# Layer 0: two units of products run one after the other, or interleaved by contraction tile

## The chip, the cores and the metric

One Trainium2 chip, one core of it. The metric is the device time of one execution of the whole program in microseconds (us), the median of several runs. Engines are named as the profile names them: PE is TensorE (PEld its weight loads), ACT is ScalarE, DVE is VectorE, POOL is GpSimd, SP is SyncE, which here issues nearly all DMAs.

## What is computed

A two-layer decoder trunk on 256 tokens of width 1024, in float32. Only the start of layer 0 matters here:

```python
xn = rms_norm(h, norm_mix_g[layer])
proj = xn @ ab_w_in[j]          # (256 x 1024) @ (1024 x 2560)
u_pool = proj[..., :256]
q, k   = the next 2 x 768 columns
v      = the last 768 columns
```

Then come pooling, six heads of differential attention, an output projection and a dense SwiGLU block; layer 1 has the same shape. All weights are read once from device memory, about 104 MB in all, so weights stream in during the whole program.

## The kernel before

**Slabs.** The host packs the weights into slabs of 128 partitions x 2048 floats (1 MB). A slab passes three places. SP loads it into one of `RAW_SLOTS = 3` raw buffers, taken in turn, so slab n can only be issued once slab n-3 has left its buffer (`sp.wait_ge(lo_ready, n-2)` in `load`). ACT rounds it to the matmul format, `w_hi` (`split_hi`, L574; parts of a slab in `part_his`, L587). DVE makes the remainder `w_lo = raw - w_hi` (`split_lo`, L1046; `part_los`, L1061) and counts `lo_ready`, which frees the raw buffer. A product takes three matmuls: hi x hi, lo x hi, hi x lo. ACT, DVE and SP each run their instructions strictly in program order; semaphore waits stand in front of the instructions that need them.

**The first two units.** `first_unit(0, 4)` makes the first 512 columns of v from slabs 0 and 1 (contraction tiles k = 0 to 3 in slab 0, 4 to 7 in slab 1) into PSUM banks 4 and 5, one per half of the tokens. `first_unit(2, 6)` makes the pool columns and the last 256 columns of v from slabs 2 and 3 into banks 6 and 7. Each step (one unit, one k) is six matmuls of 512 columns: two with `w_hi` (L1791), two with the token remainder (L1795), two with `w_lo` (L1798).

**Small pieces at the start.** Slabs 0 and 1 are loaded as three pieces of 512 columns and two of 256 (`load_first`); slabs 2 and 3 as two halves of 1024. The token columns for k = 1 to 7 come in between on the same queue (x columns: k = 1, k = 2 and 3, k = 4 to 7), and ACT (`cols_his`, L594) and DVE (`cols_los`, L1078) split them too.

**What follows.** On SP: slabs 2 to 5, the two halves of the input `h` (L499), `params`, slabs 6 to 9. On PE after the two units: `first_qk_chunk` with slabs 4 and 5, in it `rstd_rows` and `pool_transposes` (L2005), which waits for ACT to have copied the four banks 4 to 7 out (`nat_copied`, the last copy is L696). On ACT the order is slabs 4 and 5, four squares of `h` (L611), slab 6, and then those copies (L691 to L696).

Of the kernel before, what the change touches and what calls it, by code (L numbers as in the profile page):

```python
# [42 lines left out]
HALVES = 2  # L43
# [115 lines left out]
def trunk(nc, x, x_cols, norm_mix_g, norm_ffn_g, norm_final_g, params_in, slabs, out):  # L159
# [45 lines left out]
    with ctx:  # L205
# [237 lines left out]

        def part_no(s, p=0):

            return FIRST_PARTS * s + p + 1 if s < FIRST_SLABS else FIRST_SLABS * (FIRST_PARTS - 1) + s + 1

        block = ctx.enter_context(nc.Block())

# [1 line left out]
        @block.sync  # L451
        def _(sp):
            def load(n):

                key, r, free = loads[n]
                for what, count in free or ():
                    sp.wait_ge({"lo": lo_ready, "forms": forms_ready, "sum": block_sum}[what], count)
                for b in range(2):
                    c = slice(b * SLAB // 2, (b + 1) * SLAB // 2)
                    own = n < PARTED and b == 0  # L460
                    sp.dma_start(raw_of(r, c), slabs[n, :, c])\
                        .then_inc(half_loaded[n - FIRST_SLABS] if own else raw_loaded[r], 16)

            def load_first(s):

                for p in range(FIRST_PARTS):
                    c = slice(p * 512, (p + 1) * 512)
                    sp.dma_start(raw[:, s, c], slabs[s, :, c]).then_inc(first_loaded[FIRST_PARTS * s + p], 16)
                    if s == 0 and p == 0:
                        sp.dma_start(x_rest[:, 1, :], cols_of[:, 1, :]).then_inc(cols_loaded[1], 16)  # L470
                    if s == 0 and p == 1:
                        sp.dma_start(x_rest[:, 2:4, :], cols_of[:, 2:4, :]).then_inc(cols_loaded[2], 16)
                for c0 in range(FIRST_PARTS * 512, SLAB, 256):
                    sp.dma_start(raw[:, s, c0:c0 + 256], slabs[s, :, c0:c0 + 256]).then_inc(raw_loaded[s], 16)
                if s == 0:
                    sp.dma_start(x_rest[:, 4:KC, :], cols_of[:, 4:KC, :]).then_inc(cols_loaded[3], 16)

            def load_gain(st):
                g = [norm_ffn_g[0:1, :], norm_mix_g[1:2, :], norm_ffn_g[1:2, :], norm_final_g][st - 1]
                if st > 1:  # L480
                    sp.wait_ge(normed, norm_no(st))
                sp.dma_start(gain[:, :], g.broadcast_to([P, D])).then_inc(gain_loaded, 16)

            def load_all(l, part):
                for n, (key, r, free) in enumerate(loads):
                    if key[1] == l and (key[0] if key[0] in ("mix", "out") else "ffn") == part:
                        if n < FIRST_SLABS:
                            load_first(n)
                        else:
                            load(n)  # L490
                        if n == NAT[0] + 1:
                            load_x()
                            sp.dma_start(params[:, :], params_in).then_inc(params_loaded, 16)

            def load_x():

                sp.wait_ge(cols_lo, KC)
                for half in range(HALVES):
                    sp.dma_start(h[:, half, :], x[half * P:(half + 1) * P, :]).then_inc(x_loaded[half], 16)  # L499

            for l in range(2):
                load_all(l, "mix")
                load_gain(2 * l + 1)
                load_all(l, "out")
                load_all(l, "ffn")
                load_gain(2 * l + 2)
            for b in range(2):
                c = slice(b * HALFD, (b + 1) * HALFD)
                sp.wait_ge((normed, last_scaled)[b], (norm_no(4) + 1, 1)[b])
                sp.dma_start(out[0:P, c], h[:, 0, c]).then_inc(out_stored, 16)  # L510
            sp.wait_ge(normed, norm_no(4) + 2)
            sp.dma_start(out[P:2 * P, 3 * D // 4:], h[:, 1, 3 * D // 4:]).then_inc(out_stored, 16)
            sp.wait_ge(normed, norm_no(4) + 3)
            sp.wait_ge(last_scaled, 2)
            sp.dma_start(out[P:2 * P, 0:3 * D // 4], h[:, 1, 0:3 * D // 4]).then_inc(out_stored, 16)
            sp.wait_ge(out_stored, 16 * 2 * HALVES)
# [45 lines left out]
        def _(act):  # L562
            A = nc.scalar.activation

            def split_hi(s):

                r, made = preps[s]
                if FIRST_SLABS <= s < PARTED:
                    part_his(s)
                act.wait_ge(raw_loaded[r], made)  # L570
                if s >= SLOTS:
                    act.wait_ge(slab_used, s - SLOTS + 1)
                c = slice((FIRST_PARTS * 512 if s < FIRST_SLABS else SLAB // 2) if s < PARTED else 0, SLAB)
                A(w_hi[:, s % SLOTS, c], raw_of(r, c), ACT.Copy).then_inc(hi_ready, 1)  # L574
# [108 lines left out]
            def mix0_act():  # L683
# [3 lines left out]
                split_his(6)  # L687
                for half in range(HALVES):
                    act.wait_ge(pow_done, pow_no("norm", 0, half))
                    act.wait_ge(slab_used, 2)  # L690
                    A(v[:, half, 0:512], bank[:, 4 + half, :], ACT.Copy, scale=rstd[:, half:half + 1])\  # L691
                        .then_inc(nat_copied, 1)
                for half in range(HALVES):
# [318 lines left out]
            act.dma_start(first_cols, x_cols[:, 0:KC + SEQ]).then_inc(cols_loaded[0], 16)  # L1012
            act.wait_ge(consts, 1)
            A(lam_t[:, 0:1], power[:, 0:1], ACT.Copy)
            for s in range(FIRST_SLABS):
                for p in range(FIRST_PARTS):
                    if s or p:
                        cols_his(4 * s + p)
                    part_his(s, p)
                cols_his(4 * s + FIRST_PARTS)  # L1020
                split_his(s)
            split_his(2, 3)
            mix0_act()
            ffn_act(0)
# [5 lines left out]
        def _(dve):  # L1030
# [8 lines left out]

            def split_lo(s):  # L1040

                if FIRST_SLABS <= s < PARTED:
                    part_los(s)
                dve.wait_ge(hi_ready, s + 1)
                c = slice((FIRST_PARTS * 512 if s < FIRST_SLABS else SLAB // 2) if s < PARTED else 0, SLAB)
                V.tensor_tensor(w_lo[:, s % SLOTS, c], raw_of(preps[s][0], c),  # L1046
                                w_hi[:, s % SLOTS, c].bitcast(F32), ALU.subtract).then_inc(lo_ready, 1)
# [671 lines left out]
                    last_columns()  # L1719

            V.memset(ones, 1.0).then_inc(ones_made, 1)
            for s in range(FIRST_SLABS):
                for p in range(FIRST_PARTS):
                    cols_los(4 * s + p)
                    part_los(s, p)
                cols_los(4 * s + FIRST_PARTS)
                split_los(s)
            split_los(2, 3)
            mix0_dve()
            ffn_dve(0)  # L1730
# [5 lines left out]
        def _(pe):  # L1736
# [13 lines left out]
            def w_part(s, c0, n):  # L1750
                return w_hi[:, slot(s), c0:c0 + n], w_lo[:, slot(s), c0:c0 + n]
# [18 lines left out]
                if not release:  # L1770
                    last.then_inc(done, 1)

            def first_unit(s, b0):

                def split_done(parted, done, t, k):

                    if t < FIRST_SLABS and k % 4 < FIRST_PARTS:
                        pe.wait_ge(parted, part_no(t, k % 4))
                    elif k % 4 == 0:
                        pe.wait_ge(parted, part_no(t))  # L1780
                    elif k % 4 == (FIRST_PARTS if t < FIRST_SLABS else 2):
                        pe.wait_ge(done, t + 1)

                for k in range(KC):
                    t = s + k // 4
                    w1, w2 = w_part(t, (k % 4) * 512, 512)
                    if s == 0:
                        pe.wait_ge(*((cols_hi, k) if k else (col0_hi, 1)))
                    split_done(part_hi, hi_ready, t, k)
                    for half in range(HALVES):  # L1790
                        T.matmul(bank[:, b0 + half, :], xT_hi[:, half, k, :], w1, start=k == 0, stop=False)  # L1791
                    if s == 0:
                        pe.wait_ge(cols_lo, k + 1)
                    for half in range(HALVES):
                        T.matmul(bank[:, b0 + half, :], xT_lo[:, half, k, :], w1, start=False, stop=False)  # L1795
                    split_done(part_lo, lo_ready, t, k)
                    for half in range(HALVES):
                        last = T.matmul(bank[:, b0 + half, :], xT_hi[:, half, k, :], w2, start=False, stop=k == KC - 1)  # L1798
                    if k % 4 == 3:
                        last.then_inc(slab_used, 1)  # L1800

            def rstd_rows():

# [243 lines left out]
            def mix(l):  # L2047
                st, m = 2 * l, mix0[l]
                if l == 0:
                    first_unit(0, 4)  # L2050
                    first_unit(2, 6)
                else:
                    unit(m, m, 0, 4, done=nat_done, st=st)
                    unit(m + 2, m + 2, 0, 5, done=nat_done, midway=lambda: norm_transposes(st, 1))
# [323 lines left out]
```

## Time and profile before

| | |
|---|---|
| median of 3 runs | 566.34 us (566.11 to 566.46) |
| the profiled execution | 566.4 us |
| its span in the trace | 564.1 us |
| PE busy | 556.9 us, 99% of the span |
| DVE, ACT, POOL busy | 461.9, 324.3, 15.5 us |

The 2.3 us between execution and span lie outside the program's instructions. A busy share is not a limit by itself; what ends a wait is. Times below are us from the start of the span.

### The profile page before, as it was taken

Reading aid. Unit: us, or ns where it says so; the run is one execution under the profiler, and the core shown is the slowest. Engines: PE = TensorE matmul, PEld = TensorE weight load, DVE = VectorE, ACT = ScalarE, POOL = GpSimd, SP = SyncE. Lnnn points to the kernel's source line nnn. Section 1 sums busy time; section 2 is a strip of 40 time slices with the busy share of each in tenths; the row PEclk is TensorE's granted clock in tenths of the full one; section 3 lists DMA queues with packets and bytes.
Section 4 is the critical chain, followed back from the end, with each engine's and each line's share of the span. In section 5 each row is a group of like instructions: output and inputs, shape, how many; then the busy total and the mean of one; then the engine's idle time right before and its main releaser. Section 6 shows DMA issues by size and latency. Waiting matters only on the chain.

```text
span 564.1 us, 7600 instructions
## 1 busy us (share of the span) xinstructions
PE 556.9 (99%) x2949; PEld 475.1 (84%) x2949; DVE 461.9 (82%) x571; ACT 324.3 (57%) x454; POOL 15.5 (3%) x55
## 2 busy tenths in 40 slices
PE   8999999999999999999999999999999999999995
PEld 7899978888888888888888888888888888888884
DVE  5679996776988789897797998977779887798875
ACT  6686864654564555556576356546475545555543
POOL 1200001000000000000000000000000000000000
PEclk9999999999999999999999999999999999999999
DMA  8975644455627394467479622445744464926431
GB/s 297 353 298 164 217 149 145 154 195 180 223 76 243 104 314 159 145 228 255 156 242 315 226 76 74 161 146 164 273 164 140 150 223 150 304 85 215 144 112 74
DMA packets 30419, 105.65 MB, mean 187 GB/s; under 512 B 3376, under 2 KB 4272, under 8 KB 30384
## 3 DMA queue, kind: packets, MB, share of 16 engines
q1 hardware_dynamic: 30240, 105.04, 54.3%
q8 instruction: 23, 0.38, 0.3%
q10 hardware_dynamic: 144, 0.14, 0.1%
q14 instruction: 12, 0.10, 0.0%
HBM read 104.11 MB, written 1.05 MB: 186 GB/s over the span
## 4 chain that ended last, share of the span: by engine, by line
PE 97%; DMA 1%; issue 1%; DVE 1%; SPq 0%; ACT 0%; POOLq 0%; POOL 0%; DVEq 0%
PE bank L1748 20%; PE bank L1746 20%; PE bank L1747 20%; PE bank L2179 13%; PE bank L2182 7%; PE bank L1844 4%; PE bank L1847 2%; PE bank L1791 1%; PE bank L1795 1%; PE bank L1798 1%; PE bank L1816 1%; DMA raw<-in_slabs 1%; PE bank L1936 1%; PE bank L2224 1%; PE bank L1962 0%
## 5 line engine op out<-in xcount | busy, mean ns | idle before, releaser
L1046 DVE TENSOR_TENSOR w_lo<-raw,w_hi 128x2048 fp32r<-128x2048 f32 (+2 forms) x92 | 204.8, 2228 | 35.7 <-ACT w_hi L574 35.7
L574 ACT ACTIVATE w_hi<-raw 128x2048 fp32r<-128x2048 f32 (+2 forms) x83 | 153.7, 1862 | 28.6 <-DMA raw<-in_slabs 26.4
L1746 PE MATMUL bank<-w_lo,yT_hi 128*128 128x512 f32 (+1 forms) x242 | 96.1, 397 | 0.0
L1748 PE MATMUL bank<-w_hi,yT_lo 128*128 128x512 f32 (+1 forms) x242 | 94.1, 389 | 0.0
L1747 PE MATMUL bank<-w_hi,yT_hi 128*128 128x512 f32 (+1 forms) x242 | 94.0, 388 | 0.0
L2179 PE MATMUL bank<-xT,w_hi 128*128 128x512 f32 x320 | 80.5, 393 | 0.0
L2179 PEld LDWEIGHTS bank<-xT,w_hi 128*128 128x128 f32 x320 | 57.8, 189 | 10.6
L1746 PE MATMUL bank<-w_lo,xT 128*128 128x512 f32 (+1 forms) x160 | 61.9, 387 | 0.0
L1748 PE MATMUL bank<-w_hi,xT 128*128 128x512 f32 (+1 forms) x160 | 60.8, 380 | 0.0
L1747 PE MATMUL bank<-w_hi,xT 128*128 128x512 f32 (+1 forms) x160 | 60.6, 379 | 0.0
L1748 PEld LDWEIGHTS bank<-w_hi,yT_lo 128*128 128x128 f32 x242 | 45.4, 188 | 9.6
L1746 PEld LDWEIGHTS bank<-w_lo,yT_hi 128*128 128x128 f32 x242 | 45.5, 188 | 8.5 <-DVE yT_lo L1262 0.2
L1747 PEld LDWEIGHTS bank<-w_hi,yT_hi 128*128 128x128 f32 x242 | 45.6, 188 | 8.3
L2182 PEld LDWEIGHTS bank<-xT,w_lo 128*128 128x128 f32 x320 | 43.6, 190 | 3.1
L2182 PE MATMUL bank<-xT,w_lo 128*128 128x256 f32 x320 | 44.6, 282 | 0.0
L581 ACT ACTIVATE w_hi<-raw 128x2048 fp32r<-128x2048 f32 x16 | 30.7, 1917 | 21.3 <-DVE raw L1577 21.3
L1577 DVE TENSOR_TENSOR raw<-raw 128x2048 f32<-128x2048 f32 x16 | 36.5, 2284 | 0.0
L1748 PEld LDWEIGHTS bank<-w_hi,xT 128*128 128x128 f32 x160 | 30.1, 188 | 5.8
L1747 PEld LDWEIGHTS bank<-w_hi,xT 128*128 128x128 f32 x160 | 30.1, 188 | 5.3
L1746 PEld LDWEIGHTS bank<-w_lo,xT 128*128 128x128 f32 x160 | 30.1, 188 | 5.2
L1746 PE MATMUL bank<-xT,w_hi 128*128 128x256 f32 x96 | 27.6, 287 | 0.0
L1748 PE MATMUL bank<-xT,w_lo 128*128 128x256 f32 x96 | 27.2, 283 | 0.0
(229 smaller groups left out, 840.8 us busy)
## 6 DMA issues: line engine op xcount, KB each, us to landing
raw<-in_slabs SPq DMA_DIRECT2D x170, 512.0 KB, 4.7
spare<-in_slabs SPq DMA_DIRECT2D x16, 512.0 KB, 5.3
raw<-in_slabs SPq DMA_DIRECT2D x6, 256.0 KB, 6.1
h<-in_x SPq DMA_DIRECT2D x2, 512.0 KB, 8.6
gain<-in_norm_ffn_g SPq DMA_DIRECT2D x2, 512.0 KB, 7.2
raw<-in_slabs SPq DMA_DIRECT2D x4, 128.0 KB, 5.5
h<-in_x_cols SPq DMA_DIRECT2D x1, 512.0 KB, 6.3
gain<-in_norm_mix_g SPq DMA_DIRECT2D x1, 512.0 KB, 5.7
```

What stands on the lines that cost most here:

```text
L574: A(w_hi[:, s % SLOTS, c], raw_of(r, c), ACT.Copy).then_inc(hi_ready, 1)
L581: A(w_hi[:, s % SLOTS, :], raw_of(preps[s][0]), ACT.Copy).then_inc(hi_ready, 1)
L1046: V.tensor_tensor(w_lo[:, s % SLOTS, c], raw_of(preps[s][0], c), w_hi[:, s % SLOTS, c].bitcast(F32), ALU.subtract).then_inc(lo_ready, 1)
L1577: V.tensor_tensor(o, p, q, ALU.subtract).then_inc(block_sum, 1)
L1746: T.matmul(o, st_hi, mv_lo, start=first, stop=False)
L1747: T.matmul(o, st_hi, mv_hi, start=False, stop=False)
L1748: return T.matmul(o, st_lo, mv_hi, start=False, stop=last)
L1791: T.matmul(bank[:, b0 + half, :], xT_hi[:, half, k, :], w1, start=k == 0, stop=False)
L1844: T.matmul(bank[:, b, :], hi, xT[:, k, :, :, :], start=k == 0, stop=False)
L1847: last = T.matmul(bank[:, b, 0:SEQ], lo, xT_hi[:, :, k, :], start=False, stop=k == KC - 1)
L2179: T.matmul(bank[:, b + m, :], hi, xT[:, k, :, :, :], start=k == 0, stop=False)
L2182: last = T.matmul(bank[:, b + m, 0:SEQ], lo, xT_hi[:, :, k, :], start=False, stop=k == KC - 1)
```

## The change

The two units run interleaved: for each k, first the step of the v unit, then the step of the other. So the slabs are packed in another order: slab 0 is v columns k = 0 to 3, slab 1 pool and second v columns k = 0 to 3, slab 2 v columns k = 4 to 7, slab 3 the others k = 4 to 7. The small pieces of slabs 0 and 1 are loaded in turn, and ACT and DVE prepare them in turn. In the second half, the first half of slab 3 is split ahead of the second half of slab 2.

```diff
-            def load_first(s):
+            def load_first():
                 for p in range(FIRST_PARTS):
                     c = slice(p * 512, (p + 1) * 512)
-                    sp.dma_start(raw[:, s, c], slabs[s, :, c]).then_inc(first_loaded[FIRST_PARTS * s + p], 16)
-                    if s == 0 and p == 0:
+                    for s in range(FIRST_SLABS):
+                        sp.dma_start(raw[:, s, c], slabs[s, :, c]).then_inc(first_loaded[FIRST_PARTS * s + p], 16)
+                    if p == 0:
                         sp.dma_start(x_rest[:, 1, :], cols_of[:, 1, :]).then_inc(cols_loaded[1], 16)
...
-            for s in range(FIRST_SLABS):          # DVE
-                for p in range(FIRST_PARTS):
-                    cols_los(4 * s + p)
-                    part_los(s, p)
-                cols_los(4 * s + FIRST_PARTS)
-                split_los(s)
+            for p in range(FIRST_PARTS):
+                cols_los(p)
+                part_los(0, p)
+                part_los(1, p)
+            cols_los(3)
+            split_los(0, 1)
+            cols_los(4)
+            part_los(2)
+            cols_los(5, 6, 7)
+            part_los(3)
             split_los(2, 3)
...
                 for k in range(KC):
+                    for u in range(2):
+                        t, b0 = u + 2 * (k // 4), 4 + 2 * u
...
                                         # mix0_act, before the copies of banks 4 and 5
-                    act.wait_ge(slab_used, 2)
+                    act.wait_ge(slab_used, 3)
...
-            slabs += v4 + [columns(k0, 4, (w_in, 0, 256), (w_in, c_v + 512, 256)) for k0 in (0, 4)]
+            for k0, t in zip((0, 4), v4):
+                slabs += [t, columns(k0, 4, (w_in, 0, 256), (w_in, c_v + 512, 256))]
```

ACT's sequence changes in the same way as DVE's (`part_his`, `cols_his`, `split_his`). The functions `split_hi` and `split_lo` no longer call `part_his` and `part_los` for slabs 2 and 3; these stand in the sequence itself.

The order of SP's first DMAs, before (raw pieces are slab pieces, h<-in_x_cols are token columns):

```order
L468 DMA raw<-in_slabs 128x512
L470 DMA h<-in_x_cols 128x256
L468 DMA raw<-in_slabs 128x512
L472 DMA h<-in_x_cols 128x512
L468 DMA raw<-in_slabs 128x512
L474 DMA raw<-in_slabs 128x256 x2
L476 DMA h<-in_x_cols 128x1024
L468 DMA raw<-in_slabs 128x512 x3
L474 DMA raw<-in_slabs 128x256 x2
L461 DMA raw<-in_slabs 128x1024 x8
```

And of the change:

```order
L469 DMA raw<-in_slabs 128x512 x2
L471 DMA h<-in_x_cols 128x256
L469 DMA raw<-in_slabs 128x512 x2
L473 DMA h<-in_x_cols 128x512
L469 DMA raw<-in_slabs 128x512 x2
L476 DMA raw<-in_slabs 128x256 x4
L477 DMA h<-in_x_cols 128x1024
L461 DMA raw<-in_slabs 128x1024 x8
```

The same thirteen DMAs go out ahead of slab 2, but the last pieces of slab 0 have moved behind three pieces of slab 1.

DVE from the last piece of slab 0 (the first L1046 row, which frees its raw buffer) to slab 3, before:

```order
L1046 TENSOR_TENSOR w_lo<-raw,w_hi 128x512 [waits hi_ready]
L1078 SCALAR_TENSOR_TENSOR xT<-h,rows,xT 128x256 [waits cols_hi]
L1061 TENSOR_TENSOR w_lo<-raw,w_hi 128x512 [waits part_hi]
...
L1046 TENSOR_TENSOR w_lo<-raw,w_hi 128x512 [waits hi_ready]
L1061 TENSOR_TENSOR w_lo<-raw,w_hi 128x1024 [waits part_hi]
L1046 TENSOR_TENSOR w_lo<-raw,w_hi 128x1024 [waits hi_ready]
L1061 TENSOR_TENSOR w_lo<-raw,w_hi 128x1024 [waits part_hi]
L1046 TENSOR_TENSOR w_lo<-raw,w_hi 128x1024 [waits hi_ready]
```

And of the change, from the same place:

```order
L1047 TENSOR_TENSOR w_lo<-raw,w_hi 128x512 [waits hi_ready] x2
L1079 SCALAR_TENSOR_TENSOR xT<-h,rows,xT 128x256 [waits cols_hi]
L1062 TENSOR_TENSOR w_lo<-raw,w_hi 128x1024 [waits part_hi]
L1079 SCALAR_TENSOR_TENSOR xT<-h,rows,xT 128x256 [waits cols_hi] x3
L1062 TENSOR_TENSOR w_lo<-raw,w_hi 128x1024 [waits part_hi]
L1047 TENSOR_TENSOR w_lo<-raw,w_hi 128x1024 [waits hi_ready] x2
L1047 TENSOR_TENSOR w_lo<-raw,w_hi 128x2048 [waits hi_ready] x2
```

The second half of slab 2 (before: the third row with L1046; in the change: the first of the two in the row L1047 128x1024 x2) now stands behind three token columns and the first half of slab 3.

## Rows read from the trace of the kernel before

**Rows 1.** The page: busy time, share and instructions of PE.

```profile
PE 556.9 (99%) x2949; PEld 475.1 (84%) x2949; DVE 461.9 (82%) x571; ACT 324.3 (57%) x454; POOL 15.5 (3%) x55
```

**Rows 2.** Waits of PE over the whole span: total us, times, longest.

```profile
PE bank L1742 <- DVE probT L1721: 1.0, 1, 1.0
PE bank L1791 <- ACT w_hi L587: 0.4, 1, 0.4
```

**Rows 3.** Timeline of PE, 5 to 29 us: start, duration, what.

```profile
5.23 0.86 PE L1791 MATMUL bank<-w_hi,xT 128*128 128x512 f32 x2
6.39 0.63 PE L1798 MATMUL bank<-w_lo,xT 128*128 128x512 f32 x2
...
7.46 0.70 PE L1791 MATMUL bank<-w_hi,xT 128*128 128x512 f32 x2 [0.44 <-ACT w_hi L587]
8.45 0.61 PE L1798 MATMUL bank<-w_lo,xT 128*128 128x512 f32 x2
9.14 0.70 PE L1791 MATMUL bank<-w_hi,xT 128*128 128x512 f32 x2
...
10.61 0.62 PE L1791 MATMUL bank<-w_hi,xT 128*128 128x512 f32 x2
...
28.31 0.28 PE L1746 MATMUL bank<-xT,w_hi 128*128 128x256 f32 x1
```

**Rows 4.** Timeline of ACT, 4 to 19 us, where it waits for DMAs.

```profile
6.68 0.63 ACT L587 ACTIVATE w_hi<-raw 128x512 fp32r<-128x512 f32 x1 [1.20 <-DMA raw<-in_slabs]
7.71 0.51 ACT L594 ACTIVATE xT<-h,rows 128x256 fp32r<-128x256 f32 x1 [0.40 <-DMA h<-in_x_cols]
8.37 0.63 ACT L587 ACTIVATE w_hi<-raw 128x512 fp32r<-128x512 f32 x1
...
11.01 0.63 ACT L587 ACTIVATE w_hi<-raw 128x512 fp32r<-128x512 f32 x1 [0.18 <-DMA raw<-in_slabs]
...
16.99 1.06 ACT L587 ACTIVATE w_hi<-raw 128x1024 fp32r<-128x1024 f32 x1 [0.21 <-DMA raw<-in_slabs]
```

**Rows 5.** Timeline of DVE, 10 to 21 us.

```profile
10.04 0.69 DVE L1046 TENSOR_TENSOR w_lo<-raw,w_hi 128x512 fp32r<-128x512 f32 x1
...
13.29 0.48 DVE L1078 SCALAR_TENSOR_TENSOR xT<-h,rows,xT 128x256 fp32r<-128x256 f32 x1
...
16.80 1.23 DVE L1046 TENSOR_TENSOR w_lo<-raw,w_hi 128x1024 fp32r<-128x1024 f32 x1
18.08 1.23 DVE L1061 TENSOR_TENSOR w_lo<-raw,w_hi 128x1024 fp32r<-128x1024 f32 x1
```

**Rows 6.** Timeline of SP: issues of slabs 3, 4, 5, input halves.

```profile
10.75 0.33 SPq L461 DMA_DIRECT2D raw<-in_slabs  x1
15.39 0.33 SPq L461 DMA_DIRECT2D raw<-in_slabs  x1
18.06 0.33 SPq L461 DMA_DIRECT2D raw<-in_slabs  x1
18.90 0.93 SPq L499 DMA_DIRECT2D h<-in_x  x2
```

**Rows 7.** DMA view at 15.3 to 15.6: issue to landing, first half of slab 4.

```profile
raw<-in_slabs SPq DMA_DIRECT2D x1, 512.0 KB, 4.1
```

**Rows 8.** Windows: busy us of each engine, granted clock, DMA share, GB/s.

```profile
9.00:16.00 7.00, 6.92 (x31) 5.71 (x31) 6.34 (x12) 6.18 (x13) 0.88 (x5) 1.00 1.05 405
20.00:24.00 4.00, 4.00 (x19) 3.30 (x18) 1.85 (x2) 1.92 (x1) 0.28 (x3) 1.00 0.95 299
24.00:30.00 6.00, 6.00 (x35) 5.26 (x34) 3.18 (x2) 3.98 (x8) 0.00 (x0) 1.00 1.02 388
```

**Rows 9.** Timeline, 20 to 38 us: slabs 4, 5, 6 on ACT and DVE, the copies, the transposes.

```profile
20.75 1.92 ACT L574 ACTIVATE w_hi<-raw 128x2048 fp32r<-128x2048 f32 x1 [1.46 <-DMA raw<-in_slabs]
25.86 1.92 ACT L574 ACTIVATE w_hi<-raw 128x2048 fp32r<-128x2048 f32 x1 [3.19 <-DMA raw<-in_slabs]
...
27.81 2.29 DVE L1046 TENSOR_TENSOR w_lo<-raw,w_hi 128x2048 fp32r<-128x2048 f32 x1 [2.82 <-ACT w_hi L574]
...
31.18 0.28 PE L1746 MATMUL bank<-xT,w_hi 128*128 128x256 f32 x1
...
32.26 1.92 ACT L574 ACTIVATE w_hi<-raw 128x2048 fp32r<-128x2048 f32 x1 [1.54 <-DMA raw<-in_slabs]
...
36.29 0.50 ACT L696 ACTIVATE v<-bank,rstd 128x256 f32<-128x256 f32 x1
...
37.15 0.60 PE L2005 MATMUL bank<-ident,u_sb 128*128 128x128 f32 x4
```

More of the change, by code:

```diff
@@ L444, in part_no @@
         def part_no(s, p=0):
-            return FIRST_PARTS * s + p + 1 if s < FIRST_SLABS else FIRST_SLABS * (FIRST_PARTS - 1) + s + 1
+            return FIRST_SLABS * p + s + 1 if s < FIRST_SLABS else FIRST_SLABS * (FIRST_PARTS - 1) + s + 1
         block = ctx.enter_context(nc.Block())
@@ L462, in load @@
                         .then_inc(half_loaded[n - FIRST_SLABS] if own else raw_loaded[r], 16)
-            def load_first(s):
+            def load_first():
                 for p in range(FIRST_PARTS):
                     c = slice(p * 512, (p + 1) * 512)
-                    sp.dma_start(raw[:, s, c], slabs[s, :, c]).then_inc(first_loaded[FIRST_PARTS * s + p], 16)
-                    if s == 0 and p == 0:
+                    for s in range(FIRST_SLABS):
+                        sp.dma_start(raw[:, s, c], slabs[s, :, c]).then_inc(first_loaded[FIRST_PARTS * s + p], 16)
+                    if p == 0:
                         sp.dma_start(x_rest[:, 1, :], cols_of[:, 1, :]).then_inc(cols_loaded[1], 16)
-                    if s == 0 and p == 1:
+                    if p == 1:
                         sp.dma_start(x_rest[:, 2:4, :], cols_of[:, 2:4, :]).then_inc(cols_loaded[2], 16)
[L473 to L476, printed above, removed]
+                for s in range(FIRST_SLABS):
+                    for c0 in range(FIRST_PARTS * 512, SLAB, 256):
+                        sp.dma_start(raw[:, s, c0:c0 + 256], slabs[s, :, c0:c0 + 256]).then_inc(raw_loaded[s], 16)
+                sp.dma_start(x_rest[:, 4:KC, :], cols_of[:, 4:KC, :]).then_inc(cols_loaded[3], 16)
             def load_gain(st):
@@ L486, in load_all @@
                     if key[1] == l and (key[0] if key[0] in ("mix", "out") else "ffn") == part:
-                        if n < FIRST_SLABS:
-                            load_first(n)
-                        else:
+                        if n == 0:
+                            load_first()
+                        elif n >= FIRST_SLABS:
                             load(n)
@@ L567, in split_hi @@
                 r, made = preps[s]
-                if FIRST_SLABS <= s < PARTED:
-                    part_his(s)
                 act.wait_ge(raw_loaded[r], made)
@@ L1014, in _ @@
             A(lam_t[:, 0:1], power[:, 0:1], ACT.Copy)
-            for s in range(FIRST_SLABS):
-                for p in range(FIRST_PARTS):
[L1017 to L1021, printed above, removed]
+            for p in range(FIRST_PARTS):
+                if p:
+                    cols_his(p)
+                part_his(0, p)
+                part_his(1, p)
+            cols_his(3)
+            split_his(0, 1)
+            cols_his(4)
+            part_his(2)
+            cols_his(5, 6, 7)
+            part_his(3)
             split_his(2, 3)
@@ L1040, in split_lo @@
             def split_lo(s):
-                if FIRST_SLABS <= s < PARTED:
-                    part_los(s)
                 dve.wait_ge(hi_ready, s + 1)
@@ L1721, in _ @@
             V.memset(ones, 1.0).then_inc(ones_made, 1)
-            for s in range(FIRST_SLABS):
-                for p in range(FIRST_PARTS):
-                    cols_los(4 * s + p)
-                    part_los(s, p)
-                cols_los(4 * s + FIRST_PARTS)
-                split_los(s)
+            for p in range(FIRST_PARTS):
+                cols_los(p)
[7 more added lines that the diff above has]
+            part_los(3)
             split_los(2, 3)
@@ L1771, in unit, with first_units @@
                     last.then_inc(done, 1)
-            def first_unit(s, b0):
+            def first_units():
                 def split_done(parted, done, t, k):
@@ L1784, in first_unit @@
                 for k in range(KC):
[L1785 to L1800, printed above, removed]
+                    for u in range(2):
+                        t, b0 = u + 2 * (k // 4), 4 + 2 * u
+                        w1, w2 = w_part(t, (k % 4) * 512, 512)
+                        if u == 0:
+                            pe.wait_ge(*((cols_hi, k) if k else (col0_hi, 1)))
+                        split_done(part_hi, hi_ready, t, k)
+                        for half in range(HALVES):
+                            T.matmul(bank[:, b0 + half, :], xT_hi[:, half, k, :], w1, start=k == 0, stop=False)
+                        if u == 0:
+                            pe.wait_ge(cols_lo, k + 1)
+                        for half in range(HALVES):
+                            T.matmul(bank[:, b0 + half, :], xT_lo[:, half, k, :], w1, start=False, stop=False)
+                        split_done(part_lo, lo_ready, t, k)
+                        for half in range(HALVES):
+                            last = T.matmul(bank[:, b0 + half, :], xT_hi[:, half, k, :], w2, start=False,
+                                            stop=k == KC - 1)
+                        if k % 4 == 3:
+                            last.then_inc(slab_used, 1)
             def rstd_rows():
@@ L2049, in mix @@
                 if l == 0:
-                    first_unit(0, 4)
-                    first_unit(2, 6)
+                    first_units()
                 else:
```

## The prediction

> **What bounds the kernel now.** I read the page first. PE is busy for 556.9 of 564.1 us [rows 1], and the view of PE's waits has two entries in the whole span, the one before the warm-up matmuls and one of 0.4 us in the first unit [rows 2]. After 10.6 us PE never waits for anything: the kernel is PE's own work from then on, so whatever moves PE's position at one place and is not met by slack behind it arrives at the end in full. The question is only where PE stands when it leaves the changed stretch, and whether something it asks for later has become late.
>
> PE's timeline of the stretch gives the stake. The first step (one unit, one k) starts at 5.23, the second at 7.46, the third at 9.14, the fourth at 10.61, and from there 13 steps run without a gap up to 28.31, where `first_qk_chunk` starts [rows 3]. That is 17.70 / 13 = 1.36 us for a step. The first three took 5.38 us where three full-speed steps are 4.08, so the waits at the start cost 1.3 us. More than that the change can't win. PE was then short of data: ACT's timeline shows it waiting 1.20 us for the second piece of slab 0, and for token columns [rows 4]. The granted clock is 1.00 in every window I read [rows 8], which is the 2.4 GHz level, so the clock is no term.
>
> **The first eight steps of the change.** A landing depends on what stands ahead of it in SP's queue. I count the KB on SP's queue up to and with a piece and read from before when that much had landed, as ACT sees it: 640 KB at 6.68, 896 at 7.71, 1152 at 8.37, 2176 at 11.01 [rows 4]. In the new order the pieces are: slab 0 first (256), slab 1 first (512), columns k = 1 (640), slab 0 second (896), slab 1 second (1152), columns 2 and 3 (1408), and so on up to 2944 with the columns 4 to 7.
> - The second step now needs no new token columns and only the second DMA. 512 KB should land near 5.7 (estimate, between the start of the first split and 6.68). ACT takes 0.63, ready at 6.4. The first step's last pair starts at 6.39 [rows 3], so the PE is free at 6.85: no wait there.
> - It is free again at 8.2. The third step needs the second piece of slab 0: 7.71, and from ACT's start to PE's start 7.46 - 6.68 = 0.78, so 8.49. A wait of 0.3 us, and its restart costs some 0.1 more: a step after a wait took 8.45 + 0.46 - 7.46 = 1.45, not 1.36. Its end is 9.94.
> - From there there is twice the work for each token column, and all pieces are ahead: 1152 KB at 8.37 is wanted at 9.94, 1664 KB (some 9.7) at 11.3. No waits up to the end of the eighth step: 9.94 + 5 x 1.36 = 16.74.
>
> Before, eight steps ended at 10.61 + 5 x 1.36 = 17.4. So 0.67 us of the 1.3 is won up to here.
>
> **Where it is given back first.** The tenth step (second unit, k = 4) needs the first half of slab 3, which before was wanted three steps later. The ninth ends at 18.10. Slab 3 takes the raw buffer of slab 0, so its issue waits for `lo_ready` 1. Before, that was the L1046 row of 10.04, and the issue followed at 10.75 [rows 5, 6]. Now slab 0's last pieces stand behind three pieces of slab 1: 2176 KB, 11.01; ACT has the third columns to do first and ends at 12.0, DVE (behind its own third columns) at 12.7, the issue is at 12.75, 2.0 us late. That costs nothing by itself: the bytes ahead of it, through slab 2, kept the engines at 405 GB/s up to the 16 us mark [rows 8], and slab 3 landed right behind them, at 16.99 [rows 4]. I take the same landing. If the queue ran dry, its bound is the row of a transfer that met a short queue, 4.1 us from issue to landing [rows 7]: 16.85, which is no later.
>
> From 16.99: ACT 1.06 (18.05, just in time for the first pair), then DVE 1.23 [rows 5] makes its `w_lo` at 19.35 with some 0.05 for each handover. The step wants it at 18.12 + 0.91 = 19.03. A wait of 0.3 us. The remaining pair and the last six steps follow: 19.35 + 0.46 + 6 x 1.36 = 27.98. `first_qk_chunk` starts 0.33 us earlier than the 28.31 of before. That is all that is left of the gain.
>
> **Where the change makes something late.** The row to look at is DVE's order. `lo_ready` 3, which frees the buffer for slab 5, was the L1046 row of 16.80, done at 18.03, and the issue of slab 5 followed at 18.06 [rows 5, 6]. Now the second half of slab 2 stands behind token columns 5, 6, 7 (0.48 each, [rows 5]) and behind the first half of slab 3. The latter ends at 19.3, then 1.23 gives 20.52, and slab 5 is issued at 20.55: 2.5 us late. Behind it on SP's queue stand the input halves (18.90 before [rows 6]), `params` and slab 6, all late with it. Slab 4, on the other hand, goes out at 13.65 and not 15.39, but it only fills the queue sooner: bytes already asked for end at about 20.7 either way, when slab 4 reached ACT [rows 9]. So the DMA engines run dry for about a microsecond.
>
> From slab 5 through slab 6 there are six transfers of 512 KB and 291 KB, 3363 KB or 3.44 MB. The first lands 4.1 us after its issue [rows 7], at 24.65. The other 2.92 MB follow at the rate of the queue, for which I have two rows of this very stretch: 299 GB/s from 20 to 24 and 388 from 24 to 30 [rows 8]. At 388: 7.5 us, slab 6 is in at 32.2. At 299: 9.8 us, 34.4. At their mean over ten microseconds, 352: 8.3 us, 32.95. Before it was 32.26 [rows 9]. I take the mean, since the same transfers were moved at both rates and I can't say which part of the slowness comes back: slab 6 is 0.7 us late, with bounds of -0.1 and +2.15.
>
> Who waits for it? ACT reaches slab 6 after the squares of `h` and ahead of the copies of banks 4 to 7. From slab 6 on ACT to the end of the last copy it is 36.79 - 32.26 = 4.53 us, and the transposes that need that copy start on PE at 37.15, their weight load a tenth earlier [rows 9]: only about 0.25 us of slack. PE would now come at 36.7; with slab 6 at 32.95 the copies end at 37.5. PE stands there 0.8 us, and leaves 0.47 us later than before. At the bounds it leaves 0.3 us earlier, or 1.9 later.
>
> Slab 5 itself: its second half lands at 24.65 + 0.52 / 352 = 26.1; ACT 1.92 and DVE 2.29 give 30.4. The third piece of `first_qk_chunk` starts at 31.18 [rows 9], now 30.85. No wait, 0.4 us to spare; at 299 GB/s it is 30.7. The rest of the program has the same work in the same order, and PE, ACT and DVE hand to each other there, so a late PE moves them alike.
>
> A rule of the Trainium skill bears on the rate. DMA: Bandwidth & Descriptors, Specifications, gives about 358 GB/s as a core's share of HBM bandwidth. By that the 2.92 MB take 8.2 us and the sum is +0.4; it would forbid the catch-up at 388. The trace doesn't agree with it as a ceiling: seven microseconds ran at 405 GB/s [rows 8].
>
> **Sum.** -0.33 (start) + 0.80 (new wait at the transposes) = +0.47 us on the span of 564.1. The profiled execution is 566.4, the median 566.34, so they can be treated as one: 566.8. A measurement of this kernel tells about 0.2%, 1.13 us, from no change.
>
> **The rivals.**
> - *The queue catches up.* Slab 6 lands by 32.3, because the idle microsecond costs only slack. For it: from 24 us on the engines moved 388 GB/s. Against it: the slow 20 to 24 us held the same slabs. Time: 566.34 - 0.3 = 566.0, still no change. 0.20.
> - *Slower: slab 6 is very late.* The refill of the queue runs at 299 GB/s again, or slower with fewer transfers outstanding. From a landing at 33.6 on, PE's net delay passes 1.13 us; at 34.4 it is 568.2. For it: the row of 20 to 24 us is directly this traffic, and ACT waited 1.54 us for slab 6 even before [rows 9]. Slab 5's `w_lo` can add a wait, which the later one then swallows. 0.27.
> - *Faster by over 1.13 us.* The tenth step would have to find slab 3 over a microsecond sooner and slab 6 be on time; but slab 3's issue is later, not earlier. It needs nearly the whole 1.3 us. 0.06.
> - My forecast (+0.2 to +1.1): 0.47.
>
> **Numbers.** The likeliest is 566.8. The catch-up case ends at 565.9 with its scatter, and the slow one at 568.2: that is the range. Within 0.2%: 0.47 + 0.20 = 0.67; slower 0.27; faster 0.06.
>
> **What would show it.** The second step starts near 6.85, the third near 8.5; a wait of about 0.3 us in the tenth; the first `first_qk_chunk` matmul near 28.0. Slab 5's issue is at 20.5, the GB/s dips around 20 to 22 us, ACT's first row of slab 6 is near 33.0, and PE's waits have a new entry at the transposes, released by ACT's copies, of 0.8 us. It would be wrong if slab 6 came at 32.3 or at 34, if slab 3 slipped past 17.3 (each tenth then goes to the tenth step, to slab 5's issue and on), or if PE waited for slab 5.

## The result

The changed kernel takes 568.72 us (median of 6 runs, 568.26 to 569.9) against 566.28 for the kernel before (6 runs): ratio 1.0049, 95% interval 1.0039 to 1.006, so it is about half a per cent slower (the two medians alone give 2.4 us, 1.0043). I had forecast 566.8 with a range of 565.9 to 568.2. Of my cases it is the rival "Slower: slab 6 is very late", and worse than its price of 568.2.

The page of the profiled execution after (span 566.4 us, before 564.1), PE's busy time and the first groups of PE's waits (total, times, longest), to be read against [rows 1, 2]:

```profile
PE 557.6 (98%) x2949; PEld 475.1 (84%) x2949; DVE 461.5 (81%) x571; ACT 324.2 (57%) x454; POOL 15.5 (3%) x55
```

```profile
PE bank L1751 <- DVE w_lo L1047: 1.2, 1, 1.2
PE bank L1747 <- DVE probT L1722: 1.0, 1, 1.0
PE bank L1797 <- ACT w_hi L586: 0.6, 1, 0.6
PE bank L2012 <- ACT v L695: 0.2, 1, 0.2
```

The work is the same (2949 matmuls), with three new waits: 0.6 us in the tenth step, 1.2 us at slab 5's `w_lo`, 0.2 us at the transposes. The 1.0 us entry is the one before the warm-up matmuls, as before. PE's timeline places the new ones:

```profile
5.08 0.96 PE L1797 MATMUL bank<-w_hi,xT 128*128 128x512 f32 x2
...
6.80 0.62 PE L1797 MATMUL bank<-w_hi,xT 128*128 128x512 f32 x2
...
8.27 0.70 PE L1797 MATMUL bank<-w_hi,xT 128*128 128x512 f32 x2
...
9.73 0.61 PE L1797 MATMUL bank<-w_hi,xT 128*128 128x512 f32 x2
...
18.62 0.73 PE L1797 MATMUL bank<-w_hi,xT 128*128 128x512 f32 x2 [0.56 <-ACT w_hi L586]
19.19 0.63 PE L1801 MATMUL bank<-w_hi,xT 128*128 128x512 f32 x2
19.88 0.74 PE L1804 MATMUL bank<-w_lo,xT 128*128 128x512 f32 x2
...
28.64 0.28 PE L1751 MATMUL bank<-xT,w_hi 128*128 128x256 f32 x1
...
32.90 0.39 PE L1751 MATMUL bank<-xT,w_hi 128*128 128x256 f32 x1 [1.23 <-DVE w_lo L1047]
...
39.35 0.66 PE L2012 MATMUL bank<-ident,u_sb 128*128 128x128 f32 x4 [0.21 <-ACT v L695]
```

Set against before: the fourth step starts at 9.73 in place of 10.61 [rows 3], 0.9 us won, as the change meant. `first_qk_chunk` starts at 28.64 in place of 28.31: all of it, and 0.3 more, is lost in the tenth step. Its third piece starts at 32.90 in place of 31.18, the transposes at 39.35 in place of 37.15 [rows 9]. So the offsets are -0.9, +0.3, +1.7, +2.2, and the span ends 2.3 later.

What is late is seen on SP and ACT. SP's issues of slab 3 (first half), slab 5 (both halves), and ACT's first rows of slab 3's half and slabs 5 and 6:

```profile
12.59 0.33 SPq L461 DMA_DIRECT2D raw<-in_slabs  x1
...
20.98 0.33 SPq L461 DMA_DIRECT2D raw<-in_slabs  x1
21.36 1.43 SPq L461 DMA_DIRECT2D raw<-in_slabs  x1
```

```profile
17.50 1.06 ACT L586 ACTIVATE w_hi<-raw 128x1024 fp32r<-128x1024 f32 x1 [0.88 <-DMA raw<-in_slabs]
...
28.61 1.91 ACT L573 ACTIVATE w_hi<-raw 128x2048 fp32r<-128x2048 f32 x1 [4.47 <-DMA raw<-in_slabs]
...
34.77 1.92 ACT L573 ACTIVATE w_hi<-raw 128x2048 fp32r<-128x2048 f32 x1 [1.31 <-DMA raw<-in_slabs]
```

Slab 3's first half reached ACT at 17.50, not at 16.99 as before; slab 5 came at 28.61, not 25.86; slab 6 at 34.77, not 32.26 [rows 4, 9]. And the windows (busy time of the engines, granted clock, DMA share, GB/s):

```profile
14.00:16.00 2.00, 2.00 (x10) 1.65 (x10) 0.63 (x2) 1.64 (x3) 0.00 (x0) 1.00 0.97 342
...
20.00:22.00 2.00, 2.00 (x9) 1.64 (x10) 2.00 (x2) 0.46 (x1) 1.32 (x12) 1.00 0.29 102
22.00:24.00 2.00, 2.00 (x11) 1.64 (x10) 0.09 (x1) 1.77 (x1) 0.94 (x10) 1.00 0.75 244
24.00:27.00 3.00, 3.00 (x15) 2.49 (x14) 2.29 (x1) 0.15 (x1) 0.00 (x0) 1.00 0.71 213
27.00:30.00 3.00, 3.00 (x20) 2.69 (x20) 0.00 (x0) 1.39 (x1) 0.00 (x0) 1.00 1.02 398
```

The queue nearly runs dry at 20 to 22 us (102 GB/s), as forecast. But it doesn't come back at the 352 GB/s that I had reckoned with: for another five microseconds it moves 213 to 244.

A second profiled execution of each kernel was taken to see how steady this is (`changed_again` 568.52 us, `before_again` 566.17 us).

> The changed kernel, a second profiled execution. If the account of the first holds: PE waits at slab 5's w_lo (1.2 us in the first) and in the tenth step (0.6 us), slab 5 reaches ACT after 28 us. If the first was an odd execution, slab 5 reaches ACT before 27 us and PE doesn't wait for it.

> The kernel before, a second profiled execution, to see how far landings and the first steps vary from one execution to the next: slab 5 on ACT at 25.9 us within 0.5, the fourth step at 10.6 within 0.6, no wait of PE after it.

Of the changed kernel, ACT's row of slab 5 in its timeline, and then PE's waits:

```profile
28.26 1.91 ACT L573 ACTIVATE w_hi<-raw 128x2048 fp32r<-128x2048 f32 x1 [3.60 <-DMA raw<-in_slabs]
```

```profile
PE bank L1797 <- ACT w_hi L586: 1.1, 3, 0.7
...
PE bank L1751 <- DVE w_lo L1047: 0.8, 1, 0.8
PE bank L2012 <- ACT v L695: 0.2, 1, 0.2
```

The same three places wait (the L1797 entry holds two more waits of 0.2 us in the first and third steps). In the second execution of the kernel before slab 5 is on ACT at 25.43, slab 6 at 31.40, and PE's only wait besides the warm-up is one of 0.2 us at the start. From one execution of a kernel to the other these two landings move by 0.4 to 0.9 us; the 2.5 to 3.0 us by which they are later in the changed kernel don't come from that.

### The profile page after: what moved, and what is told of

It reads as the page before. It is cut to its first block, busy times and chain, and to the rows that moved or that the text cites. A ratio compares the mean times of both kernels' runs of the same rounds, so it can differ in the third digit from the quotient of the medians.

```text
span 566.4 us, 7598 instructions
## 1 busy us (share of the span) xinstructions
PE 557.6 (98%) x2949; PEld 475.1 (84%) x2949; DVE 461.5 (81%) x571; ACT 324.2 (57%) x454; POOL 15.5 (3%) x55
## 3 DMA queue, kind: packets, MB, share of 16 engines
HBM read 104.11 MB, written 1.05 MB: 186 GB/s over the span
## 4 chain that ended last, share of the span: by engine, by line
PE 91%; DMA 4%; DVE 1%; SPq 1%; issue 1%; ACT 1%; POOLq 0%; POOL 0%; DVEq 0%; ACTq 0%
PE bank L1753 20%; PE bank L1751 20%; PE bank L1752 20%; PE bank L2185 13%; PE bank L2188 7%; PE bank L1851 4%; DMA raw<-in_slabs 4%; PE bank L1854 2%; PE bank L1823 1%; PE bank L1943 1%; PE bank L2230 1%; SPq L461 1%; DVE w_lo L1062 0%; PE bank L1969 0%; PE bank L1930 0%
## 5 line engine op out<-in xcount | busy, mean ns | idle before, releaser
L1047 DVE TENSOR_TENSOR w_lo<-raw,w_hi 128x2048 fp32r<-128x2048 f32 (+2 forms) x92 | 204.8, 2229 | 37.4 <-ACT w_hi L573 37.4
L2188 PE MATMUL bank<-xT,w_lo 128*128 128x256 f32 x320 | 44.6, 282 | 0.0
L1751 PE MATMUL bank<-xT,w_hi 128*128 128x256 f32 x96 | 27.7, 288 | 1.2 <-DVE w_lo L1047 1.2
L1752 PE MATMUL bank<-xT,w_hi 128*128 128x256 f32 x96 | 27.1, 283 | 0.0
```

What stands on the lines that cost most here:

```text
L1751: T.matmul(o, st_hi, mv_lo, start=first, stop=False)
L1752: T.matmul(o, st_hi, mv_hi, start=False, stop=False)
L2188: last = T.matmul(bank[:, b + m, 0:SEQ], lo, xT_hi[:, :, k, :], start=False, stop=k == KC - 1)
```

## The experiments

Two theories stood. **Release**: the changed order of the splits frees the raw buffers of slabs 0 and 2 late, so slabs 3 and 5 are issued and land late. **Pattern**: reading the slabs in turn is itself worse for the queue or for PE. Each time below is a median with the ratio to the runs of the kernel before on the same chip (566.0 to 566.3).

**release_early**: the changed kernel with token columns 4 to 7 split ahead of slab 2, and both parts of slab 2 ahead of slab 3 (DVE in the same way).

```diff
-            cols_his(4)
-            part_his(2)
-            cols_his(5, 6, 7)
-            part_his(3)
-            split_his(2, 3)
+            cols_his(4, 5, 6, 7)
+            part_his(2)
+            split_his(2)
+            part_his(3)
+            split_his(3)
```

> The changed kernel, with one order altered: token columns 4 to 7 are split ahead of slab 2, and slab 2's second half ahead of slab 3's first half, on ACT and DVE. Theory (the late release of slab 2's raw buffer is the cause): slab 5 is issued near 18.3 us in place of 20.98, PE has no wait for slab 5's w_lo (1.2 us in the changed kernel), and the time is within 0.4 us of the kernel before, 566.0 to 566.7. Rival (interleaving and the late slab 3 cost the time): the wait for slab 3 in the tenth step stays and the time stays at 568 or more.

567.58 us, ratio 1.0027 (1.0018 to 1.0037). Slab 5 is issued at 18.09 and is on ACT at 26.45; PE has no wait at its `w_lo` and none at the transposes. So some 1.1 us of the loss is gone, as the theory wants, but not all: PE still waits in the tenth step, since slab 3's half comes at 17.70. The time expected was 566.0 to 566.7, so half of the expectation failed: I had priced that step at next to nothing.

**release_late_alone**: the kernel before, with the halves split in the changed order and nothing interleaved.

```diff
-            split_his(2, 3)
+            part_his(2)
+            part_his(3)
+            split_his(2, 3)
```

> The kernel before, not interleaved, with one order altered: the first half of slab 3 is split ahead of the second half of slab 2, on ACT and DVE, as in the change. Theory: slab 5's issue moves from 18.06 to about 20.5 us, PE gets a wait of 0.8 to 1.8 us at slab 5's w_lo or at the transposes, and the kernel is 1.3 to 2.6 us slower than before. Rival (interleaving is the cause): no new wait, within 0.3 us of before.

566.74 us, ratio 1.0015 (1.0006 to 1.0024): slower, by 0.6 us, less than half of what I expected. Slab 5 was issued at 19.87, later than before by 1.8, and reached ACT at 26.02, later by 0.16. Slab 4 isn't late there (issued at 14.83, before 15.39), the queue is back at 332 GB/s from 22 to 24 us, and PE waits for no data in the profiled execution. The late release alone, in a kernel where slab 3 is on time, costs little.

**inputs_ahead**: the changed kernel with the input halves and `params` issued ahead of slab 5.

```diff
+                        if n == NAT[0] + 1:
+                            load_x()
+                            sp.dma_start(params[:, :], params_in).then_inc(params_loaded, 16)
                         if n == 0:
                             load_first()
                         elif n >= FIRST_SLABS:
                             load(n)
-                        if n == NAT[0] + 1:
-                            load_x()
-                            sp.dma_start(params[:, :], params_in).then_inc(params_loaded, 16)
```

> The changed kernel with the two input halves and params issued ahead of slab 5, so that SP's queue has 1.3 MB to bring while slab 5 waits for its buffer. If the empty queue is what costs: the dip in GB/s at 20 to 22 us goes, slab 6 lands 1 to 2 us sooner, slab 5 too since the queue's engines are not restarted from idle, and the time falls by 0.8 us or more against the changed kernel (568.7). If the order of release alone decides (slab 5 is as late, and 1.3 MB now stand ahead of it): slab 5 lands no sooner than 28.6 and the time stays or rises.

568.81 us, ratio 1.0061 (1.0041 to 1.008). The dip is gone: 369 GB/s from 20 to 22 and 401 to 406 up to 30 us. Yet slab 5 reaches ACT at 29.17 and PE waits 1.7 us for it. The time is that of the changed kernel, where the theory of the empty queue asked for 0.8 us less: the full queue was real, and what it brought was not what PE needed next.

**pool_work_later**: POOL's constants moved behind slab 5's `w_lo` (`pool.wait_ge(lo_ready, 6)` for `cols_lo`).

> The changed kernel with POOL's 34 small writes of constants (18 to 23.5 us) moved behind slab 5's w_lo, out of the stretch in which the DMA queue runs at 150 to 270 GB/s. If POOL's writes hold up the transfers, the rate from 22 to 27 us rises to 350 or more and the time falls by about 1 us. If the slow refill has nothing to do with POOL, rate and time stay within 0.4 us of the changed kernel.

571.45 us, ratio 1.0097 (1.0083 to 1.0111), and not for the reason asked about: POOL also computes `rstd`, its writes now stand ahead of that, and PE waits 2.6 us at `rstd_rows`. What the run answers is the rate: 236 GB/s from 22 to 24 and 276 from 24 to 27 with POOL idle there, slab 5 on ACT at 28.12. So the slow refill doesn't come from POOL's writes.

**own_buffer**: the changed kernel with slab 3 in memory that is free at that time (its halves in `gain` and `xn`), outside the ring of three raw buffers. Slabs 4, 5 and 6 then wait for slabs 0, 1 and 2. **own_buffer_in_before** is the same in the kernel before.

```diff
     def slab(key):
-        r = ring.pop(0)
-        ring.append(r)
+        if len(loads) == PARTED - 1:
+            r = EARLY
+        else:
+            r = ring.pop(0)
+            ring.append(r)
...
+            if r == EARLY:
+                return gain[:, c] if c.start < SLAB // 2 else xn[:, c.start - 1024:c.stop - 1024]
```

> The changed kernel with one thing added: slab 3 goes into a buffer of its own (memory that is free at that time), so it waits for no release, and slabs 4, 5 and 6 wait for slabs 0, 1 and 2. Theory (both late releases are the cause, slab 0's for slab 3 and slab 2's for slab 5): slab 3 lands at 17.0 or sooner in place of 17.5, the wait in the tenth step falls to 0.3 us or less, slab 5 is issued by 14 us and PE never waits for it or at the transposes; the time is 565.7 to 566.2, that of before or up to 0.4 us faster. Rival (the interleaved kernel draws on the DMA queue in a worse pattern whatever the buffers do): 567 or more.

> Control: the kernel before with slab 3 in the same buffer of its own. PE waits only before its fourth step there, and slabs 3 to 5 are in time, so an earlier issue should change nothing: within 0.3 us of before. If it is faster by more, the own buffer helps by itself and the comparison of the two kernels has to be made with it in both.

The control is at 566.07 us, ratio 1.000 (0.9992 to 1.0009): the buffer does nothing by itself. The interleaved kernel with it is at 566.84 us, ratio 1.0015 (1.0007 to 1.0024): between the 565.7 to 566.2 of the theory and the 567 of its rival. Slab 5 is on ACT at 23.88 and PE waits for it nowhere. From 14 to 30 us the rate is 401 to 422 GB/s in every window of 2 or 3 us:

```profile
14.00:16.00 2.00, 2.00 (x11) 1.65 (x10) 0.05 (x1) 1.08 (x2) 0.00 (x0) 1.00 1.03 422
```

But slab 3's half, issued at 8.38 and not at 12.59, still came at 17.49, and the tenth step still waits 0.5 us. So its late issue was not the only reason: it stands behind all of slab 2 in the queue, and in this execution, the slowest of its eleven (567.75), slab 2's first half itself came 0.6 us later than in the changed kernel.

**own_buffer_halves**: that kernel with SP loading both first halves, then both second halves, and columns 4 to 7 split first.

```diff
-                        elif n >= FIRST_SLABS:
+                        elif n == FIRST_SLABS:
+                            for b in range(2):
+                                for m in range(FIRST_SLABS, PARTED):
+                                    load(m, (b,))
+                        elif n >= PARTED:
                             load(n)
```

> The interleaved kernel with slab 3 in its own buffer, SP loading the first halves of slabs 2 and 3 and then the second halves, and token columns 4 to 7 split ahead of them. Slab 3's first half should land near 15.7 us, so the tenth step has no wait at all and the whole 0.9 us won in the first eight steps reaches first_qk_chunk and the end: 565.2 to 565.5, 0.6 to 0.9 us faster than before. Rival (the win is met by a later wait, at the transposes, where the copies of the banks leave 0.25 us): 565.8 to 566.2, with a new entry in PE's waits at the transposes.

565.87 us, ratio 0.9997 (0.9988 to 1.0006): the whole loss is gone, and the gain of 0.6 to 0.9 us that I expected can't be measured. PE's timeline of this kernel, the fourth, ninth and tenth steps and the start of `first_qk_chunk`:

```profile
9.32 0.62 PE L1807 MATMUL bank<-w_hi,xT 128*128 128x512 f32 x2
...
16.37 0.70 PE L1807 MATMUL bank<-w_hi,xT 128*128 128x512 f32 x2
...
18.11 0.63 PE L1807 MATMUL bank<-w_hi,xT 128*128 128x512 f32 x2
...
27.66 0.28 PE L1761 MATMUL bank<-xT,w_hi 128*128 128x256 f32 x1
```

The fourth step is 1.29 us ahead of [rows 3]. Half of that is lost in the ninth, since slab 2's first half is on ACT only at 15.17, after a wait of 1.05 us for its DMA. At 27.66 PE is 0.65 us ahead and stays so (span 563.5). The median shows a sixth of it. The control's profiled execution was 563.5 as well: without interleaving its fourth step was 0.65 us early and its `first_qk_chunk` started at 27.67. How soon the first pieces land differs by as much between executions as the change could win. This run changes the buffer, the order of SP and the order of the splits at once; only the buffer was tried by itself.

**slab5_late_alone**: the last kernel with one wait more ahead of slab 5, `sp.wait_ge(lo_ready, 4)`.

> The kernel of own_buffer_halves with one wait added: SP issues slab 5 only when slab 3 is split (lo_ready 4, near 20.5 us), which is when the changed kernel could issue it. Nothing else is late. Theory: slab 5 reaches ACT at 28 to 28.6, PE, which comes 1 us sooner here, waits some 2 to 2.5 us for its w_lo, and the time is 567.5 to 568.5. If a late slab 5 costs less than 1 us here, the loss of the changed kernel came from the late slab 3.

566.97 us, ratio 1.0016 (1.0007 to 1.0025): 1.1 us over own_buffer_halves, less than expected. Slab 5 was issued at 20.45 after a gap of the queue (49 GB/s from 20 to 22), but was on ACT at 25.88. That is 5.4 us, where the changed kernel took 7.6 for the same two transfers. (There slab 4 was still landing, on ACT at 22.23; here it was on ACT at 20.59.) The profiled execution is one of the fastest of the eleven (566.28, the others up to 568.11): in it the late slab costs PE 0.45 us, at the transposes, and the rest of the 1.1 is seen in no trace.

**slab5_later_still**: so I made the changed kernel later. The same wait in it moves slab 5's issue from 20.98 to 22.12. The reason for choosing it was the line of the DMA view for instruction loads (queue 8: packets, MB, share of 16 engines). In the changed kernel the view of 20.9 to 22.9 us has one:

```profile
q8 instruction: 1, 0.02, 4.4%
```

4.4% of 16 engines over 2.0 us are 1.4 us of one engine, just while SP needs 1.43 us to issue slab 5's second half (a usual issue is 0.43). In slab5_late_alone the load starts at 19.5 and takes 1.0 us; none starts from 20 to 22.9.

> The changed kernel with slab 5 issued one split later (SP waits for slab 3's w_lo, near 22.1 us, in place of slab 2's, 20.98). In the changed kernel the second half of slab 5 took 1.43 us to issue, 21.36 to 22.79, during a 16 KB instruction load at 21.0 to 22.4, and then 5.8 us to land. Theory 1 (the refill of the empty queue collides with that load): issued after it, slab 5 has no long issue and lands no later than 28.7, and the time stays within 0.4 us of the changed kernel. Theory 2 (a refill with few transfers outstanding is slow wherever it falls, or the load has nothing to do with it): slab 5 lands 1.1 us later, 29.7, and the time rises by about 1 us.

568.79 us, ratio 1.0052 (1.0038 to 1.0066). SP's two issues and ACT's row in its timeline, and then the window of 24 to 27 us:

```profile
22.12 0.33 SPq L463 DMA_DIRECT2D raw<-in_slabs  x1
22.49 0.43 SPq L463 DMA_DIRECT2D raw<-in_slabs  x1
...
27.48 1.92 ACT L575 ACTIVATE w_hi<-raw 128x2048 fp32r<-128x2048 f32 x1 [2.72 <-DMA raw<-in_slabs]
```

```profile
24.00:27.00 3.00, 3.00 (x15) 2.49 (x14) 2.21 (x1) 0.76 (x1) 0.00 (x0) 1.00 0.95 329
```

Issued 1.14 us later, slab 5 arrives 1.1 us earlier. Slab 4 was on ACT only at 22.84 here, so it isn't slab 4's late landing that makes the difference. Theory 1 is borne out for the landing, with one reserve: the load runs from 20.95 to 22.33 here, so the first issue falls on its last 0.2 us. Its time is that of the changed kernel, as expected: the wait for slab 5 is down to 0.3 us, the one at the transposes is up to 0.7, so the transposes start at 38.66 in place of 39.35, and what is won is lost near the end, where PE waits 0.5 us more (below).

## Why the prediction was wrong

Its order of events was right, and the rival that names this mechanism had a chance of 0.27. Point by point:

- *The first eight steps.* Forecast: second step at 6.85, third at 8.49, fourth 0.67 us early. Measured: 6.80, 8.27, 0.88 early. Right, though part of it is the luck of early landings: the kernel before had its fourth step at 10.61, 10.38 and, with its own buffer, 9.96 in three profiled executions.
- *"That costs nothing by itself ... I take the same landing."* The first step that failed. The half landed 0.5 us late, past the 17.3 that I had named as a sign of being wrong. The tenth step lost 1.2 us in place of 0.35, and -0.33 at `first_qk_chunk` became +0.33. How much of this is the late issue is open. With slab 3 issued only at 12.6, the queue went from 412 to 342 GB/s at 14 to 16 us; but own_buffer, which issues at 8.38 and moves 422 there, has the half at 17.49. In all seven profiled executions that load it behind slab 2 in the interleaved order it is on ACT at 17.35 to 17.70; loaded ahead of slab 2's second half, in own_buffer_halves, at 16.44.
- *Slab 5 is issued 2.5 us late, at 20.55.* 20.98, since DVE came to it after the late slab 3. Right in kind.
- *"The first lands 4.1 us after its issue, the others follow at the rate of the queue."* The second step that failed, and the larger. The first half landed in 4.4 us; the second took 1.43 us to issue and 7.2 to land. Slab 5 was on ACT at 28.6, not at 26.1, so "No wait, 0.4 us to spare" became a wait that put PE 1.4 us further back. I had taken the mean of two rates; the refill ran at 213 to 244 GB/s, below both bounds. slab5_later_still shows that this is no fixed property of a refill: with the issue moved to the end of the instruction load, the same two halves took 5.4 us.
- *A wait of 0.8 us at the transposes.* The wait is there, 0.2 us, and puts PE 0.5 us further back: slab 6 came at 34.8 instead of 32.95, later than my worst bound of 34.4, but PE came late too, having waited for slab 5.
- *The sum.* Forecast -0.33 + 0.80 = +0.47. Measured +0.33 + 1.39 + 0.48 = +2.20 at the transposes, 2.3 at the end of the span, 2.4 in the medians.

How the loss splits is best read from where PE stands at the transposes in the profiled executions: 2.20 us behind [rows 9] in the changed kernel, 0.53 behind in release_early, 0.65 ahead in own_buffer_halves. So slab 5's lateness costs about 1.7 us and the late slab 3, less what the start wins, 0.5. The medians say 1.1 (changed kernel against release_early, and again slab5_late_alone against own_buffer_halves) and 1.5 (release_early against before). These two add up to the whole by construction, and release_early loses another 0.5 us near the end of the program, which belongs to neither (last section).

As a price of two microseconds the pattern theory falls: with slabs 3 and 5 in time the interleaved kernel is as fast as the other. A small part of it stands. From 8 to 10 us, ahead of any gap, all nine profiled executions with the slabs loaded in turn moved 351 to 389 GB/s, the four others 399 to 408. That is some 50 KB or 0.1 us (an estimate from these rates), and why is open. The change isn't faster, because the start it improves is only 0.9 us long and moves by 0.3 to 0.6 us from one execution to the next, and because the tenth step wants slab 3 earlier.

Open: release_late_alone costs 0.6 us at the median with no wait for data in its profiled execution. That execution can't show it: its span is 563.7 us, shorter than before's 564.1, while the eleven spans reach 566.0. That the instruction load causes the slow refill rests on its coincidence in the changed kernel, in its second execution and in pool_work_later (slab 5 on ACT 7.6, 7.2 and 7.1 us after the first issue) against 5.4 in the two kernels that issue just as such a load ends (slab5_late_alone, slab5_later_still). release_late_alone lies between: a load of 1.85 us starts at 20.8, after both halves are issued (19.87 and 20.24), and slab 5 takes 6.15 us. A kernel without the load was not tried.

## What to carry to other kernels

Before changing the order in which data is used, list for each buffer which instruction frees it and what is issued behind that in the same queue: here the DMAs kept their number and bytes, and most of the loss came from splits that moved back. A late issue can be priced at nothing only while enough is outstanding behind which the load would land anyway, so ask how much that is at that moment, and price a restart by its slow case. And when the stake is under a microsecond, look at two profiled executions of the kernel before first.

## What the runs showed of the hardware

**Transfers of 512 KB, asked for well ahead, run at 401 to 422 GB/s.** own_buffer holds this from 14 to 30 us, and own_buffer_halves 407 to 418 from 14 to 27. In the kernel before, where issues wait for buffers, some windows hold 289 to 309, in the changed one 324 to 348 before the gap. The DMA share is 93 to 97% in these slow windows and 101 to 109% in the fast ones, so a high share doesn't mean a full rate. That the number of outstanding transfers makes the difference is argued; no view counts them. The Trainium skill, DMA: Bandwidth & Descriptors, Bandwidth, advises transfers of 1 MiB or more for at least 75% of peak. This case's trace doesn't need them: the 512 KB ones ran at the 401 to 422 GB/s above. The Trainium skill, DMA: Bandwidth & Descriptors, Specifications, gives about 358 GB/s of HBM bandwidth a core; that was no ceiling in these runs of one core.

**An instruction load in the way of a lone transfer.** It showed at the end of the program too. The last slab's second half, issued at 536.18 in own_buffer, took 6.2 us to land, with one such load starting near 539.2; ACT began on it at 542.38. In the kernel before the same half, issued at 535.82, has its load two microseconds ahead of the issue, took 4.8 us and was on ACT at 540.62. A slow landing doesn't go with every load nearby, but with one that comes some two to three microseconds after the issue. Over all thirteen profiled executions: load ahead of the issue, 4.8 to 5.2 us (four); load 0.5 to 0.7 us after it, 5.1 to 5.3 (four); 1.7 us after, 5.5 (changed_again); 2.2 to 3.1 us after, 5.8 to 6.2 (release_early, pool_work_later, slab5_later_still, own_buffer, in this order). PE in own_buffer:

```profile
552.59 0.50 PE L1759 MATMUL bank<-w_lo,yT_hi 128*128 128x512 f32 x1 [0.68 <-DVE yT_lo L1556]
```

This wait of 0.3 to 0.7 us, 500 us behind the edit, stands in these last four and in no other profiled execution. From the transposes to the end of the span three of them fall back against the kernel before by 0.5 (release_early), 1.1 (own_buffer) and 0.9 us (slab5_later_still). It has nothing to do with slabs 3 and 5, so in these executions the difference to before is too large by that much; how many of the executions behind the medians have it was not seen.
